# RWKV scan of a two-block model: its 64-wide products in four quarters of the array

## The reference

```python
def step(S, inp):
    r_t, w_t, k_t, v_t, a_t, b_t = inp
    sa = jnp.einsum('bhvk,bhk->bhv', S, a_t)
    S = S * w_t[:, :, None, :] + sa[..., None] * b_t[:, :, None, :] + v_t[..., None] * k_t[:, :, None, :]
    return S, jnp.einsum('bhvk,bhk->bhv', S, r_t)
...
y = ((y - mu) * lax.rsqrt(var + RWKV_GN_EPS)).reshape(B, T, RWKV_DIM) * lnx_g + lnx_b
y = (y + bonus) * g
```

## Time and profile before

| | |
|---|---|
| median of three runs | 1838.08 us |
| the profiled execution's own time | 1841.09 us |
| its span | 1839.2 us |
| TensorE busy, share of the span | 1729.4 us, 94% |
| VectorE (DVE) | 1101.5 us, 60% |
| ScalarE (ACT) | 923.8 us, 50% |
| GpSimd (POOL) | 356.2 us, 19% |
| chain that ended last, share on TensorE | 78% |
| HBM read | 271.65 MB |

### The profile page before, as it was taken

The page is one execution under the profiler, slowest core; times in us unless marked ns, Lnnn a source line. Parts: engine busy times, 40 slices in busy tenths (PEclk is TensorE's granted clock), DMA queues, the critical chain, the costliest instruction groups (busy, mean ns, idle before and its releaser), DMA issues.

```text
span 1839.2 us, 30272 instructions
## 1 busy us (share of the span) xinstructions
PE 1729.4 (94%) x12664; PEld 1585.7 (86%) x12664; DVE 1101.5 (60%) x1737; ACT 923.8 (50%) x1434; POOL 356.2 (19%) x237
## 2 busy tenths in 40 slices
PE   6799999999989999999999997988999899989998
PEld 5789998999878999989988986867998788869986
DVE  4465655777465555558765476327544677767544
ACT  4556755665437476556644543115643444436631
POOL 0100020233020001204310444002720110006500
PEclk9899999999989999999999988859999999999999
DMA  6514345455552333545554532003555434335552
GB/s 195 173 61 160 116 158 186 161 196 183 195 164 97 135 115 134 187 160 184 184 190 158 198 119 72 25 1 129 192 206 198 172 112 153 123 115 184 187 205 89
DMA packets 45543, 274.64 MB, mean 149 GB/s; under 512 B 4704, under 2 KB 8928, under 8 KB 16224
## 3 DMA queue, kind: packets, MB, share of 16 engines
q1 hardware_dynamic: 44544, 267.18, 41.6%
q10 hardware_dynamic: 864, 5.54, 0.8%
HBM read 271.65 MB, written 1.05 MB: 148 GB/s over the span
## 4 chain that ended last, share of the span: by engine, by line
PE 78%; DVE 12%; ACT 4%; DMA 3%; issue 2%; SPq 1%; POOL 0%; DVEq 0%; ACTq 0%; POOLq 0%
PE b_ps L358 14%; PE b_ps L360 14%; PE b_ps L361 14%; PE b_ps L443 8%; PE b_ps L444 8%; PE b_ps L446 8%; DVE b_wlo L315 4%; DMA b_wraw<-in_w 3%; PE b_ps L959 2%; PE b_ps L1831 1%; ACT b_S L911 1%; PE b_ps L938 1%; ACT b_whi L307 1%; DVE b_scr L675 1%; DVE b_S L863 1%
## 5 line engine op out<-in xcount | busy, mean ns | idle before, releaser
L315 DVE TENSOR_TENSOR b_wlo<-b_wraw,b_whi 128x2048 fp32r<-128x2048 f32 (+2 forms) x266 | 582.7, 2195 | 200.8 <-PE b_ps L446 130.9
L358 PE MATMUL b_ps<-b_Hh,b_whi 128*128 128x256 f32 x2232 | 648.8, 291 | 27.3 <-DVE b_wlo L315 19.8
L360 PE MATMUL b_ps<-b_Hl,b_whi 128*128 128x256 f32 x2232 | 635.6, 285 | 0.0
L361 PE MATMUL b_ps<-b_Hh,b_wlo 128*128 128x256 f32 x2232 | 635.3, 285 | 0.0
L307 ACT ACTIVATE b_whi<-b_wraw 128x2048 fp32r<-128x2048 f32 (+2 forms) x266 | 470.7, 1771 | 229.7 <-PE b_ps L446 151.9
L358 PEld LDWEIGHTS b_ps<-b_Hh,b_whi 128*128 128x128 f32 x2232 | 432.3, 194 | 37.4 <-issue 26.1
L360 PEld LDWEIGHTS b_ps<-b_Hl,b_whi 128*128 128x128 f32 x2232 | 432.4, 194 | 1.4
L361 PEld LDWEIGHTS b_ps<-b_Hh,b_wlo 128*128 128x128 f32 x2232 | 432.2, 194 | 0.0
L1418 POOL TENSOR_TENSOR b_fl<-b_ab,b_fh 128x256 fp32r<-128x256 f32 x44 | 93.9, 2134 | 228.1 <-ACT b_fh L1391 228.1
L1473 POOL TENSOR_TENSOR b_gl<-b_relu,b_gh 128x256 fp32r<-128x256 f32 x64 | 86.9, 1365 | 135.3 <-ACT b_gh L1454 135.2
L443 PE MATMUL b_ps<-b_whi,b_gh 128*128 128x512 f32 x256 | 99.7, 389 | 0.0
(11 more groups left out here) (349 smaller groups left out, 2727.5 us busy)
## 6 DMA issues: line engine op xcount, KB each, us to landing
b_wraw<-in_w SPq DMA_DIRECT2D x223, 1024.0 KB, 4.8
b_wraw<-in_w SPq DMA_DIRECT2D x39, 512.0 KB, 3.4
b_gains<-in_gains ACTq DMA_DIRECT2D x5, 1024.0 KB, 5.1
b_bias<-in_rpb SPq DMA_DIRECT2D x8, 512.0 KB, 10.5
b_wraw<-in_w SPq DMA_DIRECT2D x2, 768.0 KB, 4.2
b_cA<-in_cA SPq DMA_DIRECT2D x2, 608.0 KB, 5.2
b_X<-in_x SPq DMA_DIRECT2D x2, 512.0 KB, 5.1
out<-b_X SPq DMA_DIRECT2D x4, 256.0 KB, 2.5
```

What stands on the lines that cost most here:

```text
L315: e.tensor_tensor(wlo[u % NLO][:, 0:n], raw[u % NRAW][:, 0:n], hi.bitcast(F32), ALU.subtract).then_inc(up("w_lo", "wlo", u))
L358: e.matmul(out, wh, x.hi[:, kk, :], start=k == 0, stop=False)
L360: e.matmul(out, wh, x.lo[:, kk, :], start=False, stop=False)
L361: ins = e.matmul(out, wl, x.hi[:, kk, :], start=False, stop=last)
```

## The change

The scan is rewritten; around it some buffers and loads move.

- The first product is cut: only what the inverse starts from (key `tn`) comes first, then the matrices of the corrections (`ta`); the products with the queries (`tr`) stand between levels 3 and 5. All have 64 columns and go to four quarters.
- Masks are multiplied in while DVE copies a product out of PSUM: no ET, no NT, none of POOL's mask products.
- Only X is carried. Its transpose is made by a product with the identity (`turned_pe`) and copied by ACT. Y is the masked product, and DVE adds px to X.
- For bs and by, corrections and values of a chunk lie in the two halves of the partitions of one buffer (VU), keys and their counterparts likewise (BKt, RKB), so one product of 128 rows replaces two of 64. The state S is 64 rows a head.
- MoBA's output projection is done in quarter steps, two a level, and six at the end.
- cW comes on the weights' queue with lora and cM into the unused second half of the gains; the first gains load is halved, the second issued after the scan. A Sqrt on a spare cell stands at the scan's start. Two rings' first buffers move into scr and spare.

```diff
-    scr = ring(top, "scr", NSCR, [P, T])
+    scrs = sb(top, "scr", [P, NSCR * T])
...
+        k = 2 if n else 1
+        e.dma_start(gains[:, 0:k, :], dram["gains"][:, n, 0:k, :]).then_inc(up("ld_g", "gains", n, by=16), 16)
...
+                    S_ring = [scrs[:, 0:384]] + ring(s2, "S", 2, [P, 384])
+                    T_ring = [spare[:, 0:384], sb(s2, "T", [P, 384])]
...
-                self.turn_tokens_act(e, w, "Vt", self.Vt)
+                for tb in range(2):
+                    w.wait_ge(*at("full", ("tok", "Vt", tb)))
+                    for c2 in range(2):
+                        r = slice(64 * c2, 64 * c2 + 64)
+                        ins = e.activation(self.VU[r, 2 * tb + c2, :], banks.tile(("tok", "Vt", tb))[r, :], ACT.Copy)
...
+        def rows_of(self, c2, par, turned):
+            r = 64 * (c2 ^ par if turned else c2)
+            return slice(r, r + 64)
+
+        QUADS = [(0, 0), (1, 1), (0, 1), (1, 0)]
+
+        def quads_pe(self, e, w, key, tbk, lhs, rhs, from_turned, to_turned, *needs):
+            bb = [banks.take(w, (key, tbk, par)) for par in range(2)]
...
+            for f in range(4):
+                for c2, par in self.QUADS:
+                    r, o = self.rows_of(c2, par, from_turned), self.rows_of(c2, par, to_turned)
+                    right = self.CW("id64")[r, :] if rhs is None else rhs[r, par, tbk, f, :]
+                    ins = e.matmul(bb[par][o, 64 * f:64 * f + 64], lhs(r, par, f), right, start=True, stop=True)
...
+        def ends_pe(self, e, w, c):
+            for f in range(4):
+                for n in range(2):
+                    o = 64 * ((c + n) % 2)
+                    ins = e.matmul(bank[o:o + 64, f * P:f * P + P], self.ends[:, n, f, 64 * c:64 * c + 64], ident, start=True, stop=True)
...
+        BESIDE = {1: ([("ob", 0)], [("ob", 1), ("ends", 0), ("ends", 1)]), 2: ([("ob", 2)], [("ob", 3), ("ends", 2), ("ends", 3)]),
+                  3: ([("ob", 4)], [("ob", 5), ("query", 0)]), 4: ([("ob", 6)], [("ob", 7), ("query", 1)]), 5: ([("ob", 8)], [("ob", 9)])}
...
+        def beside_chunk(self, c, place):
+            return {(2, 0): [0], (2, 1): [1], (2, 2): [2], (3, 0): [3], (3, 1): [4], (3, 2): [5, 6]}.get((c, place), [])
...
         def scan_pe(self, e, w):
...
+            for n in range(1, 6):
                 for tbk in range(2):
...
+                    self.grown_pe(e, w, n, tbk)
+                    self.turned_pe(e, w, n - 1, tbk)
+                self.between_pe(e, w, n, 0)
+                for tbk in range(2):
+                    self.joined_pe(e, w, n, tbk)
+                self.between_pe(e, w, n, 1)
+            for tbk in range(2):
+                self.turned_pe(e, w, 5, tbk)
...
+                for f in range(4):
+                    for par in range(2):
+                        r = self.rows_of(c2, par, True)
+                        ins = e.matmul(bu[par][flip, 64 * f:64 * f + 64], self.XT[r, par, tbk, f, :], self.Gs[r, f, :], start=True, stop=True)
...
+                            ins = e.matmul(bs[64 * par:64 * par + 64, 64 * f:64 * f + 64], self.BKt[:, c, v:v + 64], self.VU[:, c, v:v + 64], start=f == 0, stop=f == 3)
...
+                        ins = e.matmul(by[64 * par:64 * par + 64, 64 * f:64 * f + 64], self.VU[:, c, v:v + 64], self.RKB[:, par, tbk, f, c2, :],
+                                       start=c == 0 and f == 0, stop=f == 3)
...
+            for s in range(3):
+                self.norm_pe(e, w, 1, s)
+                for n in (10 + 2 * s, 11 + 2 * s):
+                    self.ob_pe(e, w, n)
...
+            self.scan_act(e, w)
             gains_act(e, w, 1)
-            self.scan_act(e, w)
...
+            e.dma_start(self.cW, dram["cW"]).then_inc(up("ld_W", "cW", by=16), 16)
...
-            e.dma_start(self.cW[:, :], dram["cW"]).then_inc(up("ld_W", "cW", by=16), 16)
...
+            e.activation(nst[:, 12:13], eps_rms, ACT.Sqrt)
...
+                        e.tensor_tensor(YY[:, par, tbk, :, :], self.by_f((f"pe{n}", tbk, par)), wide(f"lev{n}", 4), ALU.mult).then_inc(banks.free((f"pe{n}", tbk, par)))
...
+                        e.tensor_tensor(XX[:, par, tbk, :, :], XX[:, par, tbk, :, :], self.by_f((f"px{n}", tbk, par)), ALU.add).then_inc(banks.free((f"px{n}", tbk, par)))
```

More of the change, by code:

```diff
@@ L268, in program @@
     sqs = [spare[:, 0:T], spare[:, T:2 * T]]
-    scr = ring(top, "scr", NSCR, [P, T])
+    scrs = sb(top, "scr", [P, NSCR * T])
+    scr = [scrs[:, i * T:i * T + T] for i in range(NSCR)]
     STAT = 7
@@ L1818, in CW @@
             return self.cW[:, o:o + w]
[L1820 to L1838, removed]
+        def rows_of(self, c2, par, turned):
[4 more added lines that the diff above has]
+            bb = [banks.take(w, (key, tbk, par)) for par in range(2)]
+            for what in needs:
+                w.wait_ge(*at(*what))
+            for f in range(4):
[3 more added lines that the diff above has]
+                    ins = e.matmul(bb[par][o, 64 * f:64 * f + 64], lhs(r, par, f), right, start=True, stop=True)
+                    if f == 3 and (c2, par) in self.QUADS[2:]:
+                        ins.then_inc(banks.full((key, tbk, par)))
@@ new lines, in ends_act, with query_pe @@
+        def ends_act(self, e, w, c):
+            w.wait_ge(*at("full", ("bk", c)))
+            e.activation(self.BKt[:, c, :], banks.tile(("bk", c))[:, :], ACT.Copy).then_inc(banks.free(("bk", c)))
+        def query_pe(self, e, w, tbk):
+            BH, KH, AR = self.BH, self.KH, self.AR
+            bb = [banks.take(w, ("tr", tbk, par)) for par in range(2)]
+            for f in range(4):
+                for n, L in ((0, KH), (1, BH)):
+                    for c2, par in self.QUADS:
+                        c, r, o = 2 * tbk + c2, slice(64 * par, 64 * par + 64), 64 * (c2 ^ n)
+                        a = 128 * f + 64 * c2
+                        ins = e.matmul(bb[par][o:o + 64, a:a + 64], L[r, f, 64 * c:64 * c + 64], AR[r, f, c, 1, :], start=True, stop=True)
+                        if f == 3 and n == 1 and (c2, par) in self.QUADS[2:]:
+                            ins.then_inc(banks.full(("tr", tbk, par)))
@@ new lines, in query_dve @@
+        def query_dve(self, e, w, tbk):
+            for c in range(4):
+                w.wait_ge(*at("full", ("bk", c)))
+            for par in range(2):
+                w.wait_ge(*at("full", ("tr", tbk, par)))
+                out = self.RKB[:, par, tbk, :, :, :].rearrange("p f c i -> p (f c) i")
+                m = self.CW("incl").unsqueeze(1).broadcast_to([P, 8, 64])
+                e.tensor_tensor(out, banks.tile(("tr", tbk, par))[:, :].rearrange("p (g i) -> p g i", g=8), m, ALU.mult).then_inc(banks.free(("tr", tbk, par)))
@@ L1991, in scan_pe @@
-                bu = banks.take(w, ("u", c))
-                w.wait_ge(*at("free", ("g", c)))
-                w.wait_ge(*at("XT", 5, tbk))
-                for h in range(8):
-                    ins = e.matmul(bu[rows, hd(h)], self.XT[rows, h, tbk, :], self.Gs[rows, hd(h)], start=True, stop=True)
-                ins.then_inc(banks.full(("u", c)))
+                if c:
+                    for f in range(4):
+                        for par in range(2):
+                            r = slice(64 * par, 64 * par + 64)
+                            e.matmul(by[r, 64 * f:64 * f + 64], S[r, f, :], AR[r, f, c, 1, :], start=f == 0, stop=False)
@@ L2053, in scan_act @@
-            after = []
+            e.activation(nst[:, 12:13], eps_rms, ACT.Sqrt)
+            for n in range(1, 7):
+                for tbk in range(2):
+                    for par in range(2):
+                        w.wait_ge(*at("full", (f"pt{n - 1}", tbk, par)))
+                        e.activation(self.XT[:, par, tbk, :, :], self.by_f((f"pt{n - 1}", tbk, par)), ACT.Copy).then_inc(banks.free((f"pt{n - 1}", tbk, par)))
+                        sig.same(("XT", n - 1, tbk, par), ("free", (f"pt{n - 1}", tbk, par)))
+                if n < 6:
+                    self.between_act(e, w, n, 0)
+                    self.between_act(e, w, n, 1)
```

374 lines of the change are left out of this document (183 added, 191 removed).

## The result

The changed kernel takes **1789.97 us** (median of 4 runs, 1788.86 to 1792.28) against 1837.76 (median of the four runs before beside it): ratio 0.9733, 95% interval 0.9718 to 0.9748. The profiled execution took 1792.28, with a span of 1790.5, so the two profiled spans differ by 48.7 us.

What follows compares the result with a forecast made beforehand. TensorE, busy 94% of the span, was taken as the bound. Ahead +0.7, opening -8.5, levels +9.6, chunks -36.3, clock +4 and end -0.3 sum to -30.8 us: 1807 us from the median 1838.08, range 1797 to 1822.

Steps and rivals of the forecast that it cites:

- the copies of Vt: Ahead of the scan: four 64x512 copies instead of two 128x512 delay the attention's next L911, +0.7 us.
- the end of the opening: Scan's opening: DVE's 7.1 us, later than TensorE's 5.2, sets its end; -8.5 us (bounds -7.5 and -9.5).
- the levels get longer: Levels of the inverse: products, quarter steps, transposes and waits sum to 45.3 us against 35.7, +9.6 us.
- the end is 14.2 (14.4): From the last by to L584: 14.4 us against 14.7, -0.3 us.
- 27 ns for a record of four quarters: Opening and levels: a 64-column record in four quarters takes 27 ns, bounds 15 and 40, next to L1955.
- rival C: Quarter products: truly faster quarters, 20 ns a record, 9 us less, 1798 us; chance 0.12.
- -4 against before: Levels: at 15 ns a record about -4 us, since the chain of handoffs then takes over.
- 67 ns for the records of bs and by: Chunks: bs and by are 16 records each with 128 rows, 67 ns a record, 1.07 us a product.
- the clock, +4: Chunks: half clock, first expected in chunk 2, undoes part of the gain; half its cost counted, +4 us (0 to 9.5).
- after which the code is the same: From L584's start on: code unchanged, so no term in the sum for that stretch.
- quarters of 40 or 58 ns: Two rivals on quarter products: 40 ns a record, 1825 us, chance 0.08; 58 ns, 1849 us, chance 0.03.
- a clock that falls in chunks 0 and 1: Rival on the chunks: clock falls in chunk 0 or 1, 1817 us; chance 0.17.

## Why the prediction was right and wrong

**Right.** TensorE's own time bounds the scan; the alternation of shapes and the half clock were the lost time; the copies of Vt cost +0.57 (forecast +0.7); DVE sets the end of the opening (6.0, forecast 7.1), since its first mask began after 1.4 us and not 1.8, and L2199 took 1.85 and not 2.3; of the chunks, chunk 2 is where the clock falls first; the end is 14.2 (14.4). That the levels get longer holds in its direction alone (+3.4, forecast +9.6). That chunk 2 lasts 8.4 (8.3) is luck: bs and by took 1.0 us less than the 2.14 summed for them, and the half clock (0.8 on its root) and waits of 1.13 instead of 0.6 gave it back.

**Wrong: 27 ns for a record of four quarters.** This is the step that failed most. It measures 14.6, and over the 1152 records that is 14.3 us. The prediction had 15 ns as its lower bound and took 27 from L1955, "the same set of quarters". But L1955 has 128 columns; rival C named this and got a chance of 0.12. Its 28 ns times four are 112, about twice the 58 of one quarter with 64. So it was already a full fourfold overlap, if a record's time goes with its columns (one quarter alone with 128 was not run), and halving the columns halves it. L1831's 29 is likewise 58 by two. The two rows looked like one floor because twice the columns and twice the quarters cancel. The runs with the loop turned settle it: 14.6, 18.2 and 36 ns for the same records in another order. Not all of the 14.3 arrived: the levels measured 39.1, 6.2 below the forecast. The prediction's own figure for 15 ns, -4 against before, would have missed as well, by 7.4 the other way. With 16.8 for the records, 8.9 for the steps and 3.8 for the transposes, 9.6 are left over: 3.5 of "issue" (2.59 of it the stall above) and 0.5 waiting for DVE by the list of waits, and for the rest a half clock behind the stall (64 records of L1837 in 1.99 us instead of 1.16) and the changes of shape.

The Trainium skill ("TensorE: Matmul & The Clock Gate", section "Wait — 56ns, not 53.3ns?") has about 25 ns from start to start as a floor. For quarters taken in turn the trace doesn't follow it: 14.6 ns a record over 32 records, in every such product at full clock (a whole float32 matmul is two records, 29 ns). The section's figures are for back-to-back matmuls and it says nothing of tiles, so it was no ground for ruling a fourfold overlap out.

**Wrong: 67 ns for the records of bs and by.** They measure 31. The 67 came from L1980, whose eight matmuls all write one half of the columns; those of bs and by write the halves in turn. That the other rows for this (105 ns for the three loops) were mixed shapes hid it: split, L1990's own records take 39 ns in the kernel before. Chunks 0 and 1 lasted 3.8 and 3.7 us for 5.1 and 4.6.

**Mis-sized: the clock, +4.** It fell from 1180.4 to 1183.9, inside chunk 2's root and chunk 3's state part, and cost about 1.4 us (0.8 on L1927's 16 records, the rest on the 64-row products behind it). With the waits filled it didn't fall in chunk 2. The +4 was meant as half of 9.5, which is 4.75.

**Wrong: "after which the code is the same".** The code is, its banks are not. The number of banks that the scan takes sets which one its last result lies in, and that was worth 5.0 us at the MLP, 4.0 of it left at the end of the span. The changed kernel turned so that the old collision comes back loses 4.7. No view of the scan shows it; the list of waits of TensorE behind L584 does (L443 for DVE's L584), and the count of `take` calls modulo seven.

Together, in us below the forecast's stages: ahead of the scan 0.5, opening 1.1, levels 6.2, chunks and clock 5.8, end 0.2, behind L584 4.0. That is 17.8; the forecast's sum puts the span at 1808.4, and it was 1790.5. Of the rivals the one with cheaper quarters (20 ns, 1798) came nearest; quarters of 40 or 58 ns and a clock that falls in chunks 0 and 1 are refuted by the rows.

Over half of the gain in the chunks is not what the change is about. On the kernel before, splitting one loop by shape took 21.9 of the 38.1 us off the chunks in the profile, and 15.7 off the median. The Trainium skill's page "TensorEngine Tiling (Array Packing)", section "Key Properties", says that a change of tiling mode drains the engine; the trace agrees that changes cost time: 105 ns a record mixed, 35 ns apart.

## What to carry to other kernels

Before a rate is carried from a row to a new shape, write it as (time of one tile with so many columns) over (tiles at work at once), and check both factors against two rows: equal numbers can come from different factors. Issue small products in turn over the quarters or column halves, and keep one tile shape in a row; look for loops that alternate shapes before rewriting anything. When a stage changes how many buffers it takes from a ring, look at who takes the next one behind it. When a short wait is filled with work from elsewhere, look at the place that the work came from too.

## What the runs showed of the hardware

- Four 64x64 float32 quarters with 64 columns run fully at one time: 14.6 ns a record, 58 for one alone. Two column halves of 128x64 do as well: 31 ns, against 67.
- The order of issue sets how far quarters overlap: 14.6 ns with four in turn, 18.2 with two, 36 with one after another. A reach of about three records of each quarter, worked out from the 18.2, gave the 36 ahead of its run; for column halves it doesn't fit (see above).
- Mixed tile shapes cost 105 ns a record where split loops cost 35, and with them the granted clock went from 1.00 to 0.50 though TensorE counted as 96% busy ahead of the fall (12.49 of 13.00 us in the earlier trace rows). Split, it stayed at 1.00 for 12 us more.
- Stalls of 2.3 to 2.6 us on "issue" near 1138 us stand in three of the seven profiles of the changed kernel and its versions. Two of the versions have the same code up to there, and only one of them has the stall. The cause wasn't tried.
